# Split-precision unit products: five matmuls of 386, 512 and 256 columns for six of 322, and the queries' norm moved into the exponential

## What is computed

```
q, k, v = split(h @ w_qkv)
q = q * rsqrt(mean(q*q over the 64 of a head) + eps) * q_norm      # keys alike, with k_norm
s = rope(q) . rope(k) / 8 ; m = max(sink, max s)                   # latents: band of 128, plus 128 cached keys
o = sum exp(s - m) v / (exp(sink - m) + sum exp(s - m)) ;  x = x + g1 * (o @ w_o)
u = conv3(rmsnorm(x) modulated @ w_in) ; x = x + g2 * ((silu(gate) * value) @ w_out)
```

## Time and profile before

| | us |
|---|---|
| runs | 2839.80, 2840.65, 2843.64 |
| median | 2840.65 |
| the profiled execution's own time | 2844.42 |
| its span, first to last instruction | 2842.6 |
| TensorE busy (matmul) | 2742.6 |
| VectorE busy | 1573.7 |
| ScalarE busy | 1154.9 |
| GpSimd (POOL) busy | 123.2 |

### The profile page before, as it was taken

One profiled execution on the slowest core, in us unless ns is written; L12 is line 12 of the kernel. 1 busy time (PEld: TensorE's weight loads), 2 busy tenths in 40 slices (PEclk: granted clock), 3 DMA queues, 4 the chain that ended last, 5 costly groups with the idle time before them and its releaser, 6 DMA issues.

```text
span 2842.6 us, 49930 instructions
## 1 busy us (share of the span) xinstructions
PE 2742.6 (96%) x19584; PEld 2595.9 (91%) x19584; DVE 1573.7 (55%) x2665; ACT 1154.9 (41%) x1924; POOL 123.2 (4%) x151
## 2 busy tenths in 40 slices
PE   5989999999998999999899999999998999999999
PEld 4966999999998999999879999999998789999999
DVE  2678366536635664465342665366367946653662
ACT  3357354324425551343232543244244845532440
POOL 1000100000012000000201000000100010000000
PEclk8989899999999999999999999999998999999999
DMA  6123233233321433333201333233221012222222
GB/s 258 60 94 135 83 119 141 107 109 137 143 84 49 145 124 113 119 143 123 84 0 60 126 141 106 110 133 143 73 75 49 2 38 67 74 77 71 71 81 78
DMA packets 62471, 280.48 MB, mean 99 GB/s; under 512 B 7392, under 2 KB 9568, under 8 KB 49632
## 3 DMA queue, kind: packets, MB, share of 16 engines
q1 hardware_dynamic: 62304, 278.07, 27.3%
HBM read 274.88 MB, written 3.16 MB: 98 GB/s over the span
## 4 chain that ended last, share of the span: by engine, by line
PE 91%; DVE 5%; ACT 2%; issue 1%; SPq 1%; DMA 1%; POOL 0%; POOLq 0%; DVEq 0%; ACTq 0%
PE ps L513 77%; PE ps L621 3%; PE ps L716 2%; PE ps L812 2%; PE ps L702 2%; PE ps L687 1%; PE ps L571 1%; DVE prob L1329 1%; PE ps L749 1%; PE ps L579 1%; DMA first_w<-in_ada_w 1%; DVE prob L1345 1%; PE ps L549 1%; DVE h_lo L1186 1%; PE ps L795 0%
## 5 line engine op out<-in xcount | busy, mean ns | idle before, releaser
L513 PE MATMUL ps<-h_hi,w_hi 128*128 128x322 f32 x3552 | 832.5, 316 | 5.6 <-DVE h_lo L1385 1.8
L513 PE MATMUL ps<-h_lo,w_hi 128*128 128x322 f32 x3552 | 823.0, 313 | 0.0
L513 PE MATMUL ps<-h_hi,w_lo 128*128 128x322 f32 x3552 | 817.7, 311 | 0.0
L873 ACT ACTIVATE w_hi<-w_raw 128x1024 fp32r<-128x1024 f32 (+1 forms) x288 | 325.6, 1130 | 1110.4 <-PE ps L513 975.9
L513 PEld LDWEIGHTS ps<-h_hi,w_hi 128*128 128x128 f32 x3552 | 599.0, 190 | 32.1 <-issue 24.7
L513 PEld LDWEIGHTS ps<-h_lo,w_hi 128*128 128x128 f32 x3552 | 605.2, 190 | 0.0
L513 PEld LDWEIGHTS ps<-h_hi,w_lo 128*128 128x128 f32 x3552 | 604.9, 190 | 0.0
L1131 DVE TENSOR_TENSOR w_lo<-w_raw,w_hi 128x1024 fp32r<-128x1024 f32 (+1 forms) x288 | 379.0, 1316 | 118.0 <-ACT w_hi L873 116.2
L1249 DVE SCALAR_TENSOR_TENSOR x<-ps,mods,x 128x321 f32<-128x321 f32 (+5 forms) x264 | 99.8, 434 | 508.1 <-PE ps L513 508.1
L513 PE MATMUL ps<-f_hi,w_hi 128*128 128x322 f32 x1408 | 325.7, 313 | 0.0
L513 PE MATMUL ps<-f_lo,w_hi 128*128 128x322 f32 x1408 | 324.0, 311 | 0.0
(11 more groups left out here) (120 smaller groups left out, 2176.8 us busy)
## 6 DMA issues: line engine op xcount, KB each, us to landing
ada_w<-in_ada_w SPq DMA_DIRECT2D x90, 1024.0 KB, 5.3
w_raw<-in_w_in SPq DMA_DIRECT2D x176, 512.0 KB, 3.2
w_raw<-in_w_out SPq DMA_DIRECT2D x64, 704.0 KB, 4.0
w_raw<-in_w_qkv SPq DMA_DIRECT2D x24, 512.0 KB, 3.2
w_raw<-in_w_o SPq DMA_DIRECT2D x16, 512.0 KB, 3.2
first_w<-in_ada_w SPq DMA_DIRECT2D x6, 1024.0 KB, 15.3
w_raw<-in_w_fnet SPq DMA_DIRECT2D x8, 512.0 KB, 3.3
x<-in_x SPq DMA_DIRECT2D x1, 2576.0 KB, 10.2
```

The source lines that it names most:

```text
L513: mm = pe.matmul(ps[:, 2 * par + hf, 0:NH], w[par][:, kk, :], b[:, hf * NH:(hf + 1) * NH], start=(kk == 0 and n == 0), stop=(kk == k - 1 a ...
L873: act.activation(w_hi[par][:, 0:k, :], w_raw[par][:, 0:k, :], ACT.Copy).then_inc(hi_made, 1)
```

## The change

The layout: the two shift columns move into the gaps (columns 0 and 513), so 642 columns remain. The high and low parts of a k-tile lie side by side in one tensor `h[P, 8, 2, 642]` (and `f`). A k-tile is five matmuls: 386 columns (`MAIN`) for each of the three products, into bank 2*par; high weights times the last 256 columns (`TAIL`) of the high and the low part in one matmul of 2 x 256 columns, into the two halves of bank 2*par+1; and low weights times the last 256 columns of the high part. The two halves of that bank have to be added: ScalarE copies the second half to SBUF (`tail_copy`, ahead of `split_hi`), and VectorE adds the first (`add_tails`) within `rescale` and `update`.

The queries: their sums of squares are still made, but the root is kept per tile, token block and head (`query_root`, on ScalarE), its inverse is the scale of the exponential (`exps`) and of the maximum (`masked`), and the sink column is multiplied by the root (POOL). The query gain goes into the rotary tables (`query_tables`, once per attention layer, after the keys) and, for the context tokens, into one multiplication (`query`). `turn_heads` and `invert` remain for the two key tiles only. The V transposes follow units 5 and 8, their copies precede the rescales of units 6 and 9. The last query's sums come after the first two scores, its rotation after `masked` of the first work item.

```diff
-NT = 644
-NH = NT // 2
+NT = 642
+TAIL = 256
+MAIN = NT - TAIL
...
-        h_hi = sb("h_hi", [P, KT, NT], F32R)
-        h_lo = sb("h_lo", [P, KT, NT], F32R)
+        h = sb("h", [P, KT, 2, NT], F32R)
+        h_hi, h_lo = h[:, :, 0, :], h[:, :, 1, :]
...
# POOL
-            for hx in (h_hi, h_lo):
-                for a0, n in PADS:
-                    pool.memset(hx[:, :, a0:a0 + n].bitcast(F32), 0.0).then_inc(setup_done, 1)
...
-                            pool.tensor_copy(prob[w % 3][:, :, end:end + 1].rearrange("p h c -> p (h c)"),
-                                             sink_col[:, a, head:head + 5:4]).then_inc(sink_put, 1)
+                            pool.wait_ge(q_root, KT * a + tile + 1)
+                            pool.tensor_tensor(prob[w % 3][:, :, end:end + 1].rearrange("p h c -> p (h c)"),
+                                               sink[:, a, head:head + 5:4], q_rms[:, tile, nb, :],
+                                               ALU.mult).then_inc(sink_put, 1)
...
# TensorE
+            def products(par, kk, b, first, last):
+                main, wide = ps[:, 2 * par, 0:MAIN], ps[:, 2 * par + 1, :]
+                wh, wl = w_hi[par][:, kk, :], w_lo[par][:, kk, :]
+                pe.matmul(main, wh, b[:, 0, 0:MAIN], start=first, stop=False)
+                pe.matmul(main, wh, b[:, 1, 0:MAIN], start=False, stop=False)
+                pe.matmul(wide, wh, b[:, :, MAIN:NT], start=first, stop=last, skip_group_check=True)
+                pe.matmul(main, wl, b[:, 0, 0:MAIN], start=False, stop=last)
+                return pe.matmul(wide[:, 0:TAIL], wl, b[:, 0, MAIN:NT], start=False, stop=last,
+                                 skip_group_check=True)
...
-                    b_hi, b_lo = rhs(kk)
-                    for n, (w, b) in enumerate(((w_hi, b_hi), (w_hi, b_lo), (w_lo, b_hi))):
-                        for hf in range(2):
-                            mm = pe.matmul(ps[:, 2 * par + hf, 0:NH], w[par][:, kk, :],
-                                           b[:, hf * NH:(hf + 1) * NH],
-                                           start=(kk == 0 and n == 0), stop=(kk == k - 1 and n == 2))
+                    mm = products(par, kk, rhs(kk), kk == 0, kk == k - 1)
...
                 if i:
-                    pe.wait_ge(qk_normed, 10 * a + i)
+                    pe.wait_ge(qk_normed, 2 * a + min(i, 2))
+                if i >= 3:
+                    pe.wait_ge(q_root, KT * a + i - 2)
...
-                        if n >= 3:
+                        if n in (3, 4):
                             turn_heads(layer, n - 3)
-                    sum_heads(layer, 9)
...
+                        if n in (5, 8):
+                            v = (n - 5) // 3
+                            pe.wait_ge(qkv_out, 12 * a + v + 1)
+                            if v or a:
+                                pe.wait_ge(v_ready, 2 * a + v)
+                            for tb in range(5):
+                                at = TOKEN_BLOCKS[tb]
+                                mm = pe.transpose(ps[:, 6 + tb // 4, (tb % 4) * P:(tb % 4 + 1) * P],
+                                                  qkv[:, V0 + v, at:at + P], ident[:])
+                            mm.then_inc(v_turned, 1)
...
+                        if w - w0 < 2:
+                            wait_taken(pe, u0 + 10 + w - w0)
...
+                        if w == w0:
+                            sum_heads(layer, 9)
...
# ScalarE
+            def tail_copy(u, par):
+                act.wait_ge(unit_done, u + 1)
+                act.activation(tail_low[par][:], ps[:, 2 * par + 1, TAIL:2 * TAIL], ACT.Copy).then_inc(tail_copied, 1)
...
+            def query_root(a, tile):
+                act.wait_ge(heads_summed, 10 * a + tile + 3)
+                act.activation(q_rms[:, tile, :, :],
+                               ps[:, INV_CTX, SUMS].rearrange("p (b c) -> p b c", c=2), ACT.Sqrt,
+                               bias=eps_wide[:, 0:1], scale=1.0).then_inc(q_root, 1)
...
-                                           bias=st[:, 1:2], scale=HD ** -0.5,
+                                           bias=st[:, 1:2], scale=q_scale[:, tile, nb, hd:hd + 1],
...
# VectorE
+            def add_tails(u, par):
+                dve.wait_ge(tail_copied, u + 1)
+                dve.tensor_tensor(tail[par][:], ps[:, 2 * par + 1, 0:TAIL], tail_low[par][:],
+                                  ALU.add).then_inc(tail_added, 1)
+                dve.wait_ge(tail_added, u + 1)
...
-                dve.tensor_tensor(halves(scaled[par][:]), product(par), halves(rstd[:]),
+                dve.tensor_tensor(scaled[par][:, 0:MAIN], ps[:, 2 * par, 0:MAIN], rstd[:, 0:MAIN], ALU.mult)
+                add_tails(u, par)
+                dve.tensor_tensor(scaled[par][:, MAIN:NT], tail[par][:], rstd[:, MAIN:NT],
                                   ALU.mult).then_inc(taken[par], 1)
...
-                for at, n, bank, col, cnd in ((1, NH - 1, 0, 1, 0), (NH, LAT + 1 - NH, 1, 0, 0),
-                                              (CTX0, CTX, 1, CTX0 - NH, 1)):
+                for at, n, src, cnd in ((LAT0, MAIN - LAT0, ps[:, 2 * par, LAT0:MAIN], 0),
+                                        (MAIN, LAT0 + LAT - MAIN, tail[par][:, 0:LAT0 + LAT - MAIN], 0),
+                                        (CTX0, CTX, tail[par][:, CTX0 - MAIN:NT - MAIN], 1)):
+                    if at == MAIN:
+                        add_tails(u, par)
...
+                    def query(tile):
+                        n = Q0 + tile
+                        dve.wait_ge(q_root, KT * a + tile + 1)
+                        dve.reciprocal(q_scale[:, tile, :, :], q_rms[:, tile, :, :]).then_inc(q_inv, 1)
+                        dve.wait_ge(qkv_out, 12 * a + n + 1)
+                        prompt = qkv[:, n, CTX0:CTX0 + CTX]
+                        dve.tensor_scalar(prompt, prompt, head_gain[:, a, 0:1], None, ALU.mult)
+                        dve.wait_ge(q_inv, KT * a + tile + 1)
+                        dve.tensor_scalar(neg_scale[:, tile, :, :], q_scale[:, tile, :, :], -1.0, None,
+                                          ALU.mult).then_inc(q_scaled, 1)
+                        turn_pairs(qkv[:, n, LAT0:LAT0 + LAT])
...
-                        if n >= 3:
+                        if n in (3, 4):
                             rotate(n - 3)
+                        if n == 4:
+                            query_tables()
+                        if n > 4:
+                            query(n - 5)
...
                         if w < w0 + 40:
                             masked(w)
+                        if w == w0:
+                            query(KT - 1)
```

More of the change, by code:

```diff
@@ L58 @@
 ROW_COLS = 32
-SH0 = NT - 2
+SHIFT_AT = (0, CTX0 - 1)
+SHIFTS = slice(0, CTX0, CTX0 - 1)
 UNIT0 = [sum(MIX_UNITS[k] + FFN_UNITS for k in KINDS[:i]) for i in range(DEPTH + 1)]
 SQ0 = [sum(2 * KT + (10 if k == "attn" else 0) for k in KINDS[:i]) for i in range(DEPTH)]
-RMS0 = [sum(2 + (10 if k == "attn" else 0) for k in KINDS[:i]) for i in range(DEPTH)]
+RMS0 = [sum(2 + (2 if k == "attn" else 0) for k in KINDS[:i]) for i in range(DEPTH)]
 HFREE0 = [(KT - 1) * sum(k != "pool" for k in KINDS[:i]) for i in range(DEPTH)]
@@ L276, in rms_base @@
         def rms_base(layer, second):
-            return RMS0[layer] + (1 + (10 if KINDS[layer] == "attn" else 0) if second else 0)
+            return RMS0[layer] + (1 + (2 if KINDS[layer] == "attn" else 0) if second else 0)
         def last_update(layer, second, kk):
@@ L482, in _ @@
                         w0 = 40 * a
-                        pool.wait_ge(sink_scaled, 1)
+                        if layer == 0:
+                            pool.wait_ge(const_in, 16 * len(CONSTS))
                         pool.wait_ge(qkv_out, 12 * (a + 1))
@@ L546, in tile @@
                     pe.wait_ge(hl_made, low_base(layer, second) + kk + 1)
-                    for n, (w, b) in enumerate(((w_hi, h_hi), (w_hi, h_lo), (w_lo, h_hi))):
-                        for hf in range(2):
-                            mm = pe.matmul(ps[:, 2 * s + hf, 0:NH], w[s][:, kk, :],
-                                           b[:, kk, hf * NH:(hf + 1) * NH],
-                                           start=(kk == 0 and n == 0), stop=(kk == KT - 1 and n == 2))
+                    mm = products(s, kk, h_tiles(kk), kk == 0, kk == KT - 1)
                     if kk == KT - 1:
@@ L927, in gained @@
                             act.wait_ge(unit_done, UNIT0[layer] + MIX_UNITS[KINDS[layer]])
-                    act.activation(h_hi[:, kk, SH0:NT], mods[layer % 2][:, shift + kk, :], ACT.Copy)
+                    act.activation(h_hi[:, kk, SHIFTS], mods[layer % 2][:, shift + kk, :], ACT.Copy)
                     for at, n, cnd in STREAMS:
@@ L986, in _ @@
                         op.then_inc(qkv_out, 1)
-                    root(RMS0[layer] + 10, heads_summed, 10 * (a + 1), 1.0 / HD, 2)
+                    query_root(a, KT - 1)
                     w0 = 40 * a
```

(10 more changed lines are left out.)

97 lines of the change are left out of this document (53 added, 44 removed).

## The result

The changed kernel takes 2819.51 us (2818.01 to 2822.06 in four runs); the kernel before, run beside it, 2841.53. The ratio is 0.9923, with a 95% interval of 0.9908 to 0.9939: 22 us faster. The forecast was 2790 us, in a range of 2774 to 2812, so the change earned less than half of what was forecast, and the range missed it.

A forecast was written before the change was run, and what follows sets the result against it. The prediction took TensorE's unit products, 77% of the chain, as the bound; -48.2 - 4.4 - 10.4 + 4.5 + 5 + 0.5 + 2 = -51.0 us gave 2790 us from a median of 2840.65, range 2774 to 2812.

The forecast's parts named there:

- Unit products: TensorE's k-tiles: five matmuls for six save 19.3 ns each over 2,496 k-tiles, -48.2 us; bounds -43 to -58.
- the -6: Unit products: the gain in us if only columns were saved, 2.5 ns a k-tile.
- rival (C): Copy and waits make VectorE and ScalarE the bound in last layer, norms and loop: 2806 to 2812 us; chance 0.14.
- +2: Last layer's up units: lateness per pair from added VectorE and ScalarE work, partly absorbed by buffers; us, of 0 to 10.
- Norms: Eight norms: the x update in the chain becomes 0.45 us longer; +5 us, from +2 to +10.
- Queries' norm and transition: Attention layers: fewer norm turns in qkv units, -4.4 us, and shorter TensorE idle before the first probability turn, -10.4 us.
- The loop's term: Attention loop: the exponential's per-partition scale costs ScalarE 0.19 us per work item; +4.5 us, from 0 to 15.
- (A): Unit products: the 15 ns belong to weight changes or banks, which five matmuls keep; 2826 us, chance 0.05.
- (B): Unit products: narrow matmul uncovers the weight load or the two-run read stalls; +170, 2960 us, chance 0.10.
- (D): Queries' norm: the first turn waits as long as before, behind the last query's rotation; 2800 us, chance 0.10.
- The forecast's mark of error: Unit products: forecast wrong if the distance after the narrow matmul exceeds 140 ns or after the joint one 250.

The follow-up runs named there:

- e2: Changed kernel with the joint 512-column matmul made as two of 256 columns; 2829.66 us (0.9955 of the kernel before).
- m2: e5 with four matmuls a k-tile (512, 512, 390, 512 columns; result not the reference's); 2786.36 us (0.9807).
- v1: Changed kernel with two narrow matmuls into the same columns, no copy or add, only in units whose copy stands on the path; 2810.32 us (0.9885).
- e5: Changed kernel without ScalarE's tail copy and VectorE's addition (one product missing in the result); 2803.38 us (0.9862).
- e3: Changed kernel back to six matmuls of 322 columns, without copy and add, keeping the queries' part; 2827.45 us (0.9952).
- m3: e3 with its six matmuls ordered by bank, so the bank changes once per three; 2825.66 us (0.9944).
- m4: m2 with a tile of zeros from elsewhere in memory streamed in all unit products; 2800.57 us (0.9853).
- e6: Changed kernel with the exponential's scale a constant again instead of an operand; 2819.70 us (0.9925).
- e1: Changed kernel with the joint matmul reading 512 columns in one run instead of two of 256; 2822.37 us (0.9929).

## Why the prediction was wrong

**Unit products: half right in mechanism, and mis-sized; this is the step that failed.** The text says "14 to 15 ns come with each matmul, not with its columns", and draws a line through 149.1 ns at 322 columns and 227.1 at 512. The first point is that of the units. The second was taken from one line, L812, while the other 512-column line of the same trace, L795, had 232. The distances in units, measured: 121 at 256 columns, 149 at 322, 176 at 386, 180 at 390, 232 at 512. These means lie within 1.5 ns of 7.3 + 0.440 x columns (120.0, 149.0, 177.1, 178.9, 232.6). So of the 15 ns above N / 2.4 GHz at 322 columns, half is a price of the matmul and half grows with its columns. At equal columns a removed matmul gives back 4.3 ns (e2 to the changed kernel) or 7.1 (the changed kernel to m2), not 15. The k-tile fell by 10.8 ns (11.9 with the turns) and not by 19.3: -27 to -30 us in place of -48.2. This term alone is off by about 20 us of the 25 that the sum is off against the profiled pair (-51 and -26.4). It lay outside its own bounds too: these ran from -43 to -58, and the -6, though named, wasn't kept; two points from different code left both the price and the slope free.

The Trainium skill ("TensorE: Matmul & The Clock Gate", "Back-to-back issue gap") gives N / 2.4 + 2.5 ns for a single matmul's gap and, for a stream with weight loads, about 131 ns at N = 512. The trace agrees with neither: 232 ns at 512.

**Last layer: rival (C), in one of the three places that it named.** The working had the pair at 14.6 us against 14.0 and up to 6 us of lateness in a half, then let buffers absorb 4 of them and took +2. The pair did take 14.5, and the leg lost 9 us: 5.4 in the two runs of up units, 3.9 in the two of down units, which begin with the wait for the last of `f`. v1 and e5 show the cause by taking it away. The value between 0 and 10 that was taken was the wrong end: here, where the chain of the other two engines is longer than TensorE's, the lateness was not absorbed but only postponed.

**Norms: the number came, in part by luck.** +5 forecast. Beside the products the stages around the norms gained 0.6 us in layer 0 and lost 2.0, 0.4 and 3.9 after it, +5.7. The largest, layer 2's, is the clock that fell. That is not the added work: e5, without the copies, has the same fall, and its fourth leg is as long (771.0 against 770.9 us). The three kernels with products of 322 columns (before, e3, m3) were granted 1.00 over 1540 to 1580 us, all others 0.91 or, m4, 0.96; the waits there were 1.85 to 1.91 us in the first and 1.98 to 2.97 in the others. What in the new form of the products sets the fall off stays open.

**Queries' norm and transition: right in kind, a little small.** Expected -14.8 with turns and transitions, and +4.5 in the loop. The loop's term was 0 (e6): ScalarE was "full" there only in the sense that nothing waited for it long. The first and fourth legs gained some 8 us beside their products, with the norm's loss of 4 in the fourth: -12 for the attention layers; e3 alone gives -15. Part of it is clock: at the start of the loop the low clock held for 10.2 us in place of 17.1, in layer 3 and in layer 0, which is worth at most 3.4 us each. How much of the transition is that and how much the order of the rotations was not separated.

**Rivals.** (A)'s time, 2826, is nearer than the forecast, and its ground, no full price per matmul, is half right; its mechanism (banks, weight changes) is not (m3). (B) and (D) fell to e1, e2 and e3. The forecast's mark of error (over 140 ns after the narrow matmul, over 250 after the joint one) was too coarse to see 5 ns on each wide matmul, and those 5 ns decided.

## What to carry to other kernels

A saving of so many nanoseconds on every one of thousands of matmuls rests on a slope: take its points from the same loop, and when two lines of the trace show one width at two distances, keep both as bounds. Count what merging matmuls saves from widths measured in place (here 4 to 7 ns for each one less), not from the excess over the clock. And when a helper engine gets work "under cover", compare its pair time with TensorE's where both run longest without a break: half a microsecond per pair of units came out as 9 us in one layer, and giving only those units the other form won it back.

## What was not expected of the hardware

- The distance of fp32r matmuls, each with its own 128x128 weight load, was 7.3 ns plus 0.440 ns a column from 256 to 512 columns; columns alone at 2.4 GHz would be 0.417.
- A moving operand read in two runs of 256 columns 642 elements apart costs nothing (232.1 ns in one run, 232.6 in two), and a 256-column matmul hides a weight load shown as 189 ns.
- One line of 512-column products stands 227 ns apart, another and the units 232 in the mean; neither the values nor other engines' work explained it. In units it goes with the part of the tensor that is streamed: 227.6 ns at one k-tile, 237.4 at another, in every layer alike, and 233 to 234 everywhere when all stream one tile of zeros.
- At the norm of layer 2 some 7 us at the low clock came with every kernel whose unit products were not the 322-column ones (3 us in m4), with waits of 1.98 to 2.97 us, and with none of the three that had those, with waits of 1.85 to 1.91 us.
